# Sparse attention: where the queries of heads 8 to 15 leave their banks, and where one weight split stands

## What is computed

```python
def nsa_mixer(u, table, w_in, ...):            # 16 heads of 64, in 4 groups
    q, kc, vc, ks, vs, kw, vw, gate, z = jnp.split(u @ w_in, points, axis=-1)
    q = q.reshape(b, s, G, J, dh) * (dh ** -0.5)
    ...                                        # k_cmp, v_cmp: 31 compressed keys and values
    p_c = softmax(q @ k_cmp + bias_c)          # compressed branch
    p_s = softmax(q @ k_g + bias_s)            # selected blocks: here all 8 of 8 blocks
    p_w = softmax(q @ k_win + bias_w)          # window of 512: here the whole past
    o = gate_0 * (p_c @ v_cmp) + gate_1 * (p_s @ v_g) + gate_2 * (p_w @ v_win)
    return (o * silu(z)) @ w_out
```

## Time and profile before

| | |
|---|---|
| time, median of 3 runs | 2127.84 us (2125.84 to 2128.97) |
| the profiled execution | 2125.84 us, its span 2124.5 us |
| TensorE busy | 2053.8 us, 97% of the span |
| DVE, ACT, POOL busy | 965.3 us (45%), 778.9 us (37%), 321.6 us (15%) |
| mean granted TensorE clock | 0.992 of full speed |

### The profile page before, as it was taken

The page is one execution under the profiler, slowest core; times in us unless marked ns, Lnnn a source line. Parts: engine busy times, 40 slices in busy tenths (PEclk is TensorE's granted clock), DMA queues, the critical chain, the costliest instruction groups (busy, mean ns, idle before and its releaser), DMA issues. The chain is left out here.

```text
span 2124.5 us, 26709 instructions
## 1 busy us (share of the span) xinstructions
PE 2053.8 (97%) x10149; PEld 1661.8 (78%) x10149; DVE 965.3 (45%) x1967; ACT 778.9 (37%) x1557; POOL 321.6 (15%) x489
## 2 busy tenths in 40 slices
PE   5999999999999999999999999989998999899998
PEld 4787887888888886688888888868787888677766
DVE  3427344433354344535533443354435664535445
ACT  3225332222223222333322222233336884324453
POOL 1103110000001120000110000022003764402311
PEclk9999999999999999999999999999999999999999
DMA  4431132333324331133243333225322102323212
GB/s 139 120 96 31 50 122 82 98 99 99 91 79 139 99 94 56 46 93 100 70 129 99 95 94 99 89 70 175 99 79 60 32 22 100 100 82 100 70 50 80
DMA packets 96767, 187.32 MB, mean 88 GB/s; under 512 B 8408, under 2 KB 16640, under 8 KB 96513
## 3 DMA queue, kind: packets, MB, share of 16 engines
q1 hardware_dynamic: 90288, 164.35, 25.5%
q0 software_dynamic: 6352, 21.27, 3.1%
HBM read 181.33 MB, written 4.26 MB: 87 GB/s over the span
## 5 line engine op out<-in xcount | busy, mean ns | idle before, releaser
L1895 DVE TENSOR_TENSOR wl<-raw,wh 128x1024 fp32r<-128x1024 f32 x306 | 374.7, 1230 | 782.5 <-ACT wh L1353 781.7
L1353 ACT ACTIVATE wh<-raw 128x1024 fp32r<-128x1024 f32 x306 | 320.8, 1053 | 835.9 <-PE bank L729 802.8
L729 PE MATMUL bank<-hTh,wh 128*128 128x512 f32 (+2 forms) x1200 | 467.5, 390 | 0.2 <-issue 0.2
L729 PE MATMUL bank<-hTl,wh 128*128 128x512 f32 (+2 forms) x1200 | 467.0, 389 | 0.0
L729 PE MATMUL bank<-hTh,wl 128*128 128x512 f32 (+2 forms) x1200 | 466.8, 389 | 0.0
L729 PEld LDWEIGHTS bank<-hTh,wh 128*128 128x128 f32 (+2 forms) x1200 | 223.9, 187 | 48.5 <-issue 0.3
L729 PEld LDWEIGHTS bank<-hTh,wl 128*128 128x128 f32 (+2 forms) x1200 | 223.9, 187 | 48.4
L729 PEld LDWEIGHTS bank<-hTl,wh 128*128 128x128 f32 (+2 forms) x1200 | 223.9, 187 | 47.9
L729 PE MATMUL bank<-wh,hTh 128*128 128x512 f32 x400 | 156.5, 391 | 0.1
L729 PE MATMUL bank<-wh,hTl 128*128 128x512 f32 x400 | 155.7, 389 | 0.0
L729 PE MATMUL bank<-wl,hTh 128*128 128x512 f32 x400 | 155.6, 389 | 0.0
(11 more groups left out here) (368 smaller groups left out, 3110.0 us busy)
## 6 DMA issues: line engine op xcount, KB each, us to landing
raw<-in_ffn_w_in SPq DMA_DIRECT2D x88, 512.0 KB, 3.6
raw<-in_ret_w_in SPq DMA_DIRECT2D x48, 512.0 KB, 3.8
raw<-in_ffn_w_out SPq DMA_DIRECT2D x44, 512.0 KB, 3.7
raw<-in_diff_w_in SPq DMA_DIRECT2D x32, 512.0 KB, 3.7
raw<-in_fox_w_in SPq DMA_DIRECT2D x24, 512.0 KB, 3.8
raw<-in_nsa_w_in SPq DMA_DIRECT2D x20, 512.0 KB, 3.7
raw<-in_ret_w_out SPq DMA_DIRECT2D x16, 512.0 KB, 3.7
raw<-in_fox_w_out SPq DMA_DIRECT2D x8, 512.0 KB, 3.6
```

The lines of the kernel that those rows point to most:

```text
L729: i = pe.do.matmul(dst, x, y, start=first and k == 0 and q == 0, stop=stop)
L1353: act.do.activation(M.hl[n % HL_SLOTS][0][:, 0:m], M.raw[n % RAW_SLOTS][:, 0:m], ACT.Copy).then_inc(*T.up("act_hi", n))
L1895: dve.do.tensor_tensor(wl[:, 0:m], M.raw[n % RAW_SLOTS][:, 0:m], wh[:, 0:m].bitcast(F32), ALU.subtract).then_inc(*T.up("dve_lo", n))
```

## The change

Passes 4 to 7 no longer stand beside the product `nsa q4`. Pass 4 stands behind tile 1, pass 5 behind tile 3, pass 6 behind tile 5 and pass 7 behind tile 7, on ACT and on DVE. They are staged in `pT[4]` and `pT[5]` in place of `xn`, which the first tiles use, and each waits for the pass ahead of it. The fourth split of `nsa q4` comes behind tile 16 on both engines. The copies that first write `pT[4]` and `pT[5]` wait for pass 7. TensorE, POOL and SP have the same lists as before, and no instruction is added or removed.

```diff
+def late_query(n):
+
+    return [4 + n // 2] if n in (1, 3, 5, 7) else []
+
+
+def query_stage(M, t):
+
+    a = M.nsa
+    if t >= 4:
+        return a.pT[4][:, :, :].rearrange("p k c -> p (k c)"), a.pT[5][:, :, :].rearrange("p k c -> p (k c)")
+    return tuple(x[:, t % 2 * S:t % 2 * S + S] for x in M.xn)
...
+    def take_q(t):
+        base, o = t // 4 * 4, t % 4
+        r, before = 64 * (t // 2 % 2), t - (1 if base else 2)
+        hi, _ = query_stage(M, t)
+        act.wait_ge(*at("pe_product", (f"nsa q{base}", o)))
+        act.wait_ge(*at("pe_cmp", ("hidden", 1)))
+        if before >= base:
+            act.wait_ge(*at("act_q", before))
+            act.wait_ge(*at("dve_qlo", before))
...
-    act_product(act, T, M, 4, 4, take_q(0))
-    act_product(act, T, M, 4, 4, take_q(4))
+    act_product(act, T, M, 4, 4, take_q)
+    act_product(act, T, M, 3)
...
             act.wait_ge(*at("pe_pt", ("nsa", n)))
+            if n == 4:
+                act.wait_ge(*at("act_q", 7))
+                act.wait_ge(*at("dve_qlo", 7))
...
     for n in range(128 + 10):
         if n < 128:
             exp(n)
+        for t in late_query(n):
+            take_q(t)
+        if n == 16:
+            act_split(act, T, M)
         if 0 <= n - 6 < 128:
             turned_out(n - 6)
...
-    dve_product(dve, T, M, 4, 4, take_q(0))
-    dve_product(dve, T, M, 4, 4, take_q(4))
+    dve_product(dve, T, M, 4, 4, take_q)
+    dve_product(dve, T, M, 3)
...
             dve.wait_ge(*at("pe_pt", ("nsa", n)))
+            if n == 5:
+                dve.wait_ge(*at("dve_q", 7))
...
             largest(n)
         if 0 <= n - 1 < 128:
             total(n - 1)
+        for t in late_query(n):
+            take_q(t)
+        if n == 16:
+            dve_split(dve, T, M)
```

More of the change, by code:

```diff
@@ L1678, in hidden @@
         act.do.activation(a.hid[:, w, :], M.bank[bank["nsa hidden", w]][:, 0:124], ACT.Silu, bias=a.pev[:, w:w + 1]).then_inc(*up("act_hid", w))
[L1680 to L1695, removed]
+    def take_q(t):
[7 more added lines that the diff above has]
+            act.wait_ge(*at("dve_qlo", before))
+        act.do.activation(hi.bitcast(F32R), M.bank[bank[f"nsa q{base}"][o]][:, :], ACT.Copy, scale=0.125).then_inc(*up("act_qhi", t))
+        act.wait_ge(*at("act_qhi", t))
+        for par in range(2):
+            act.do.activation(query(M, 2 * t + par)[r:r + 64, :], hi[64 * par:64 * par + 64, :], ACT.Copy).then_inc(*up("act_q", t))
     act_product(act, T, M, 4, 4, take_c)
@@ L2343, in pev, with take_q @@
         dve.do.tensor_copy(a.pev[:, w:w + 1], M.bank[bank["nsa hidden", w]][:, 124:125]).then_inc(*up("dve_pev", w))
[L2345 to L2358, removed]
+    def take_q(t):
+        base, o = t // 4 * 4, t % 4
+        r, before = 64 * (t // 2 % 2), t - (1 if base else 2)
+        hi, lo = query_stage(M, t)
+        dve.wait_ge(*at("act_qhi", t))
+        if before >= base:
+            dve.wait_ge(*at("dve_q", before))
+        dve.do.scalar_tensor_tensor(out=lo, in0=M.bank[bank[f"nsa q{base}"][o]][:, :], scalar=0.125, in1=hi, op0=ALU.mult,
+                                    op1=ALU.subtract).then_inc(*up("dve_qlo", t))
+        dve.wait_ge(*at("dve_qlo", t))
+        for par in range(2):
+            dve.do.tensor_copy(query(M, 2 * t + par)[64 - r:128 - r, :], lo[64 * par:64 * par + 64, :]).then_inc(*up("dve_q", t))
     dve_by_tile(dve, T, M, take_v, late=("n4", {1: (2,), 2: (3,)}))
```

## The result

The changed kernel takes 2135.24 us (median of 6 runs, 2132.25 to 2137.92), the kernel before 2126.76 us (6 runs, 2125.72 to 2128.97): 8.5 us more, a ratio of 1.0038 with a 95% interval of 1.0028 to 1.0049. The forecast was 2135.4 us, a shift of 7.6 us on a median of 2127.84 us, and slower by over 0.2% with a chance of 0.77. The profiled execution of the changed kernel is the fastest of its six, 2132.25 us (span 2130.9).

What follows compares the result with a forecast made beforehand. The prediction took the filling phase to be bound by a chain of ACT and DVE, not TensorE. It summed 4.1 (passes) + 2.0 (split) + 1.5 (clock) = +7.6 us on 2127.84, giving 2135.4 us, range 2130.5 to 2139.0.

Steps and rivals of the forecast that it cites:

- Tile 0, 5.74 us earlier: Start of the attention: DVE reaches tile 0 at 1612.48, no longer behind passes 4 to 7 and the split.
- A pass costs 2.24 us until DVE is free, and 2.46 in all: Between the first tiles: each of four late passes delays the chain, 9.85 us added in all.
- the walk: Filling phase, timed instruction by instruction: copy of turned tile 1 at 1630.29 against 1626.19, a shift of +4.1 us.
- The split, +2.0 us: At tile 16: TensorE stops 2.0 us for the copy of turned tile 11, delayed by the split; bounds 0 and 2.9.
- The clock, +1.5 us: After TensorE's idle pieces: at least one more stretch at 1.2 GHz while TensorE is full; bounds 0 and 4.
- The passes fit in: Filling phase: passes fill times when DVE and ACT would wait; 5.7 us less, 2122.1 us; chance 0.07.
- a pass costs only ACT's time: Filling phase: the late passes shift the end by only +1.5 us, 2129.3 us; chance 0.06.
- The split and the clock cost nothing: First phase shifts as walked, the delay at tile 16 ends in slack; +4.1 us, 2131.9 us; chance 0.20.
- The clock stays down longer: Idle pieces and the tile 16 stop hold TensorE at 1.2 GHz in several stretches; +10.1, 2137.9 us; chance 0.13.
- Copies and POOL collide: DVE's pass copies are held by POOL's tile weighing, 3.1 us more, 2138.5 us; chance 0.04.

Runs made afterwards that it cites:

- passes-alone kernel: The changed kernel with the split moved from tile 16 to behind the attention; 2131.76 us against 2127.07 for the kernel before, ratio 1.0020.
- split-alone kernel: The kernel before, its passes untouched, with the split put at tile 16; 2129.32 us against 2127.07 for the kernel before, ratio 1.0009.

## Why the prediction was right

- **The number: right, with some luck.** The shift was 8.5 us, and 7.6 were forecast. The forecast stood on a median of three runs, 2127.84 us, and the median of six was 1.1 us lower; the two errors cancel, and so 2135.4 stands beside 2135.24. For the profiled execution the same sum gave 2133.4 us, and it was 2132.25.
- **Tile 0, 5.74 us earlier: right.** DVE starts it at 1612.60, against 1618.22 and the forecast of 1612.48; the product ended 0.17 us later in this execution.
- **A pass costs 2.24 us until DVE is free, and 2.46 in all: right.** All four distances from a pass on ACT to the next tile on DVE are 2.24 us. The passes start at 1615.08, 1619.96, 1624.02 and 1628.58, each 0.10 to 0.19 us behind the walk, and the copy of turned tile 1 at 1630.49 against 1630.29. The turn of tile 3 comes 4.14 us later after the first scores, where 4.1 were forecast. In the passes-alone kernel's attention this is 4.29, and 4.7 in its median.
- **The split, +2.0 us: the mechanism right, the size a little high.** The stop is 0.18 + 1.45 us. The chain is the one forecast: ACT's half, DVE's half, tile 17, its exponential, the copy of turned tile 11.
- **The clock, +1.5 us: right as a mean, not as a fixed amount.** By the table it is about nothing in the first profile of the changed kernel, 2.7 us in the second (1.3 of them ahead of the stop), and 2.9 in the split-alone kernel. The first profile is of the fastest of six executions and the second of the slowest of five, so the mean of the two, 1.35 us, says little on the common one. The medians put the two last terms at 3.5 us together (2135.24 less 2131.76), or 3.8 if each is taken against the kernel before in its own rounds; forecast were 2.0 + 1.5. Of this 1.6 is the stop. That the other 1.9 to 2.2 us are the clock is read from the profiles; the medians do not show in which stage they lie. The clock of 0.50 while TensorE still waits in pieces for ACT and DVE, from 1618 to 1630, costs nothing that the copy of turned tile 1 shows: its shift is the walk's. Only what is left of it once TensorE is full costs time. The prediction did not set what is left of it in the two kernels against each other, and there it was lucky: the kernel before runs 3.4 us at 1.2 GHz behind its last wait and the changed one 3.8, so the two nearly cancel (12.0 and 12.16 us in the table). Against a kernel without that second fall, as with the split behind the attention (10.57), it would have been 1.6 us.
- **The rivals.** "The passes fit in" needed a price below 1.44 us a pass; the kernel with DVE's half one tile later shows that even then 1.45 us of some 4.3 come back, no more. That kernel is also what "a pass costs only ACT's time" describes, and it comes out 1.88 us late at the turn of tile 3, where the changed kernel comes out 4.14 us late. "The split and the clock cost nothing" falls with the split-alone kernel, but comes nearly true when the halves are two tiles apart (+0.5 us in the attention, 0.6 in the median). "The clock stays down longer", 2137.9 us, is what the slowest executions of the changed kernel show (2137.92 and 2137.45 us), and not the median. "Copies and POOL collide" did not happen: DVE's copies take 0.87 to 0.88 us as before, and in the first pass POOL's 0.45 us at 1615.17 are over before the copies start at 1616.41; in the last, its 0.77 us at 1628.10 are over by 1628.87, and the copies start at 1629.91. The Trainium skill's rule that a DVE copy in a two-port mode and a GpSimd instruction exclude each other (SBUF — State Buffer, section Who interferes with whom) is neither borne out nor refuted here, as the copies of the four passes and POOL's work never met.
- **What the prediction did not see** is that the kernel before had its own loss: without the early split its attention is 3.3 us shorter in both profiles, 1.8 of them in the chain to the turn of tile 3 and 1.4 of the clock. In the medians it is only 0.6 to 0.7 us, inside the intervals. No version here is faster than the kernel before by more than the measurement tells.

## What to carry to other kernels

Moving an instruction from beside a long product to between the first tiles is not a move from one idle place to another: here the filling pipeline was a chain through ACT and DVE, and what was put into it was paid in full. Price such a step by the distance to the next instruction that waits (2.24 us here, and 2.46 with what that instruction then delays), not by the engine's own time (1.8). If a two-engine step must stand in a full pipeline, try its halves some tiles apart; the same two instructions cost 3.5 us together and 0.6 us two tiles apart, and no other distance was tried. A stop of TensorE in a full stretch can cost more than its idle time: 1.6 us of idle time went with 3.5 us in the medians, and in two of three profiles the clock added 1.4 and 2.9 us. And when a change is priced by the shift of a chain, look at the clock behind its end in both kernels: the time at 1.2 GHz there is part of the price.

## What was not expected of the hardware

- The same stop of 0.18 + 1.45 us left the granted clock at 1.00 in one execution and brought it to 0.55 and 0.59 in two stretches of 2 us in another of the same program. In a third, the split-alone kernel, it was 0.50 for 4 us. One profile of such a stop is no measure of it.
- With a column of 4 bytes a partition allocated ahead of the operands of 1056 matmuls, these stood 234 ns apart in place of 229 (5 us in all). An experiment that allocates anything should compare the untouched stages first.
- A dummy exponential moved the table load of 1.28 us out of the chain, though ACT had been idle just ahead of it, and the attention became 1.17 us shorter. Whether that kernel, without the 5 us of the column, would beat the one before wasn't tried.
